# A decoder layer in float32: in the down projection, 19 low weight parts come from accumulating DMAs and 13 places, not 10, use Strassen's seven products

## The reference

```python
h = rms_norm(x); proj = h @ w_in                       # 2048 x 9216
y_a = multiscale_pool(...) @ w_branch_a
y_b = hgrn2(...) @ w_branch_b
x = x + (sigmoid(gate_a) * y_a + sigmoid(gate_b) * y_b) @ w_out
u = causal_depthwise_conv(rms_norm(x) @ w_up)          # 2 x 5504 columns
u_gate, u_val = split(u)
x = x + (silu(u_gate) * u_val) @ w_down                # 5504 x 2048: the down projection
x = x + sigmoid(rms_norm(x) @ w_ple_gate) * (p @ w_ple)
return rms_norm(x)
```

## Time and profile before

| | |
|---|---|
| median of 3 runs | 1424.06 us (1424.05 to 1424.47) |
| the profiled execution | 1424.01 us, of which the span is 1422.1 us |
| granted TensorE clock, mean | 0.998 of full |
| TensorE busy | 1412.8 us, 99% of the span |
| VectorE busy | 1070.7 us, 75% |
| ScalarE busy | 789.3 us, 56% |
| GpSimd busy | 133.6 us, 9% |
| HBM read | 270.53 MB, 192 GB/s over the span |

### The profile page before, as it was taken

How to read it: one execution, slowest core, us unless ns; L and a number is a source line. 1 busy time by engine, 2 the same in 40 slices (tenths; PEclk the granted TensorE clock), 3 DMA queues, 4 the chain that set the end, 5 groups by cost and what they waited for, 6 DMA issues and landing times.

```text
span 1422.1 us, 19817 instructions
## 1 busy us (share of the span) xinstructions
PE 1412.8 (99%) x7060; PEld 1200.5 (84%) x7060; DVE 1070.7 (75%) x1354; ACT 789.3 (56%) x959; POOL 133.6 (9%) x87
## 2 busy tenths in 40 slices
PE   9999999999999999999999999999999999999997
PEld 8888888888888888888888888888888888888886
DVE  7676777878787888777777777777777888887755
ACT  7565665555455555455555555555555555555544
POOL 0024123100000000001110111101111000000000
PEclk9999999999999999999999999999999999999999
DMA  9665554565666675475656556566665556565653
GB/s 327 198 182 160 169 185 149 164 191 176 196 210 186 216 239 195 152 222 178 200 177 198 187 182 197 179 199 184 185 194 181 201 193 206 172 218 191 233 199 120
DMA packets 190877, 273.48 MB, mean 192 GB/s; under 512 B 11744, under 2 KB 103136, under 8 KB 190688
## 3 DMA queue, kind: packets, MB, share of 16 engines
q1 hardware_dynamic: 190384, 272.30, 59.8%
q10 hardware_dynamic: 432, 0.37, 0.1%
HBM read 270.53 MB, written 2.10 MB: 192 GB/s over the span
## 4 chain that ended last, share of the span: by engine, by line
PE 98%; DVE 1%; issue 0%; ACT 0%; ACTq 0%; POOLq 0%; POOL 0%; DVEq 0%
PE aux L933 11%; PE main L933 11%; PE main L718 10%; PE main L720 10%; PE main L719 10%; PE aux L942 6%; PE main L942 6%; PE main L776 5%; PE main L777 5%; PE main L778 5%; PE aux L776 4%; PE aux L777 4%; PE aux L778 4%; PE aux L720 2%; PE aux L718 2%; PE aux L719 2%
## 5 line engine op out<-in xcount | busy, mean ns | idle before, releaser
L1552 DVE TENSOR_TENSOR w_lo<-raw,w_hi 128x1024 fp32r<-128x1024 f32 (+1 forms) x478 | 583.9, 1235 | 291.3 <-ACT w_hi L1226 290.2
L1226 ACT ACTIVATE w_hi<-raw 128x1024 fp32r<-128x1024 f32 (+1 forms) x478 | 501.4, 1051 | 462.8 <-PE main L720 126.8
L718 PE MATMUL main<-w_hi,xT 128*128 128x512 f32 x510 | 200.7, 394 | 0.0
L719 PE MATMUL main<-w_lo,xT 128*128 128x512 f32 x510 | 198.6, 389 | 0.0
L720 PE MATMUL main<-w_hi,xT 128*128 128x512 f32 x510 | 198.5, 389 | 0.0
L933 PE MATMUL aux<-xT,w_hi 128*128 128x512 f32 x704 | 169.7, 391 | 0.0
L933 PE MATMUL main<-xT,w_hi 128*128 128x512 f32 x672 | 162.8, 391 | 0.0
L933 PEld LDWEIGHTS aux<-xT,w_hi 128*128 128x128 f32 x704 | 129.4, 188 | 25.1
L933 PEld LDWEIGHTS main<-xT,w_hi 128*128 128x128 f32 x672 | 123.2, 188 | 23.6
L720 PEld LDWEIGHTS main<-w_hi,xT 128*128 128x128 f32 x510 | 95.7, 188 | 20.0
L718 PEld LDWEIGHTS main<-w_hi,xT 128*128 128x128 f32 x510 | 95.8, 188 | 19.7 <-DVE xT L1579 0.4
(11 more groups left out here) (347 smaller groups left out, 2167.7 us busy)
## 6 DMA issues: line engine op xcount, KB each, us to landing
raw<-in_w_up SPq DMA_DIRECT2D x336, 256.0 KB
raw<-in_w_in SPq DMA_DIRECT2D x136, 512.0 KB
raw<-in_w_down SPq DMA_DIRECT2D x84, 512.0 KB
raw<-in_w_out SPq DMA_DIRECT2D x32, 512.0 KB
raw<-in_w_ple_gate SPq DMA_DIRECT2D x32, 512.0 KB
raw<-in_w_branch_a SPq DMA_DIRECT2D x16, 512.0 KB
raw<-in_w_branch_b SPq DMA_DIRECT2D x16, 512.0 KB
raw<-in_w_in SPq DMA_DIRECT2D x15, 256.0 KB, 5.6
```

The lines of the kernel that those rows point to most:

```text
L718: pe.matmul(acc, th, wh, start=first, stop=False)
L719: pe.matmul(acc, th, wl, start=False, stop=False)
L1226: ac.activation(w_hi[:, u % RING, :, 0:w], raw[:, u % RING, :, 0:w], ACT.Copy).then_inc(hi_full, 1)
L1552: dve.tensor_tensor(w_lo[:, u % RING, :, 0:w], raw[:, u % RING, :, 0:w], w_hi[:, u % RING, :, 0:w].bitcast(F32), ALU.subtract).then_inc(lo ...
```

## The change

Three things change, all in the down projection. `SEVEN_AT` gets 13 places instead of 10. Of the plain units with a = 1, 19 (`LO_BY_DMA`: local numbers 13, 17, 19, 23, 27, 29, 33, 37, 39 and 53, 57, 59, 63, 67, 71, 73, 77, 81, 83) no longer get their low part from VectorE. For these, ScalarE first writes the negated high part into a buffer of its own, `w_lo_more`, two deep; then a DMA issued by GpSimd reads the same weights a second time from HBM and adds them onto it. TensorE waits for that DMA (`lo_arrived`). SyncE may refill the ring place of such a unit as soon as its high part is made. The size of a scratch area for the DMA descriptors of GpSimd is set, too.

```diff
-SEVEN_AT = ((5, 8, 11, 14, 17), (5, 8, 11, 14, 17))
+SEVEN_AT = ((5, 7, 10, 12, 15, 17), (3, 5, 8, 10, 12, 15, 17))
...
+LO_BY_DMA = [down_unit(p, i, 1) for p in range(2) for i in range(6 - 2 * p, 20) if i not in SEVEN_AT[p]]
+def lo_split(u):
+    return u + 1 - sum(v <= u for v in LO_BY_DMA)
...
+        w_lo_more = sb("w_lo_more", [P, 2, 2, NCOL], F32R, ffn)
...
+        def lo_arrived(eng, u, it=None):
+            if it is None and u in LO_BY_DMA:
+                k = LO_BY_DMA.index(u)
+                eng.wait_ge(hi_full, u + 1)
+                eng.wait_ge(lo_added[k % 2], 16 * (k // 2 + 1))
+            else:
+                eng.wait_ge(lo_full, plus(lo_split(u), 2 * UK, it))
...
             def slot_split(u, it=None):
                 if u >= RING:
-                    sp.wait_ge(lo_full, plus(u - RING + 1, 2 * UK, it))
+                    if it is None and u - RING in LO_BY_DMA:
+                        sp.wait_ge(hi_full, u - RING + 1)
+                    else:
+                        lo_arrived(sp, u - RING, it)
...
             def down_plain(u, p, i, a):
-                pe.wait_ge(lo_full, u + 1)
+                lo_arrived(pe, u)
...
             def split_hi(u, it=None):
                 ac.wait_ge(raw_full[u % RING], plus(32 * (u // RING + 1), 32 * (2 * UK // RING), it))
+                if it is None and u in LO_BY_DMA:
+                    k = LO_BY_DMA.index(u)
+                    if k > 1:
+                        ac.wait_ge(units_done, LO_BY_DMA[k - 2] + 1)
+                    ac.activation(w_lo_more[:, k % 2], raw[:, u % RING], ACT.Copy, scale=-1.0).then_inc(hi_negated, 1)
                 if u >= RING:
                     ac.wait_ge(units_done, plus(u - RING + 1, 2 * UK, it))
...
             def split_lo(u, it=None):
-                if u >= UNITS:
+                if u >= UNITS or (it is None and u in LO_BY_DMA):
                     return
...
+            for k, u in enumerate(LO_BY_DMA):
+                p, i = divmod((u - DOWN) // 2, UD)
+                pool.wait_ge(hi_negated, k + 1)
+                pool.dma_start(w_lo_more[:, k % 2], w_down_v[:, 2 * i:2 * i + 2, (2 * p + 1) * NCOL:(2 * p + 2) * NCOL],
+                               accum_op=ALU.add).then_inc(lo_added[k % 2], 16)
             root(2)
...
-    nc = bacc.Bacc("TRN2", target_bir_lowering=False, num_devices=1)
+    nc = bacc.Bacc("TRN2", target_bir_lowering=False, num_devices=1, dynamic_dma_scratch_size=8192)
```

More of the change, by code:

```diff
@@ L367, in build @@
         lo_full = sem("lo_full")
+        hi_negated, lo_added = sem("hi_negated"), [sem(f"lo_added{r}") for r in range(2)]
         units_done = sem("units_done")
@@ L722, in unit @@
             def unit(u, c, i, n, hi, lo, k, it=None, width=NCOL, tiles=2):
-                pe.wait_ge(lo_full, plus(u + 1, 2 * UK, it))
+                lo_arrived(pe, u, it)
                 for a in range(tiles):
@@ L787, in ring_tile @@
             def ring_tile(u, t):
-                return w_hi[:, u % RING, t, :], w_lo[:, u % RING, t, :]
+                low = w_lo_more[:, LO_BY_DMA.index(u) % 2, t, :] if u in LO_BY_DMA else w_lo[:, u % RING, t, :]
+                return w_hi[:, u % RING, t, :], low
             def sum_tile(q, t):
@@ L1186, in _ @@
                 for j in range(SPLIT_TB):
-                    pe.wait_ge(lo_full, u + j + 1)
+                    lo_arrived(pe, u + j)
                     for a in range(2):
@@ L1193, in _ @@
                     main_released(c - 1)
-                pe.wait_ge(lo_full, u + SPLIT_TB + 1)
+                lo_arrived(pe, u + SPLIT_TB)
                 if tb == 0:
```

## The result

The changed kernel takes 1473.88 us (median of 4 runs, 1469.45 to 1474.01) beside 1424.10 us for the kernel before: a ratio of 1.0341, 95% interval 1.0329 to 1.0354. That is 49.8 us slower, where 5 us slower was forecast. The profiled execution is the shortest of the four: 1469.45 us, a span of 1467.6 us, 45.4 us over the one before.

The account below looks back on a forecast made before the run. TensorE, busy 99%, alone was taken to bound the down projection. The terms -2.04 + 0.1 + 1.1 + 6.0 gave about +5 us on 1424.01, so 1429.1 us, range 1422.0 to 1440 (the forecast's own 1426.9 to 1437).

Parts of the forecast that it names:

- The accumulating DMA: the term that decides: Down projection, 19 units: DMA takes 6.0 us (4.1 load, 1.3 reading SBUF, 0.6 descriptors and sharing), adding +6.0 us in all.
- The upper bound of the same paragraph: Accumulating DMA behind or between two loads of a burst takes as long as three loads together, 8.3 us.
- The time that TensorE leaves: From negated copy to TensorE's start: 5.35 us at 13 units behind a place, 5.9 us at six second pairs.
- They don't add in full: Latenesses of 8.5 and 0.6 us partly overlap, as VectorE and loads gain during waits; two thirds kept, +6.0 us.
- the four units named beforehand: Units 17, 53, 57 and 71, where TensorE's largest waits for the accumulating DMA were expected; waits of 0.3 to 1.3 us.
- VectorE's load: Down projection: VectorE's total hardly moves, -2 us, but changed order costs 0.1 at one spot and +1.2 us together at others.
- in time: Rival: the DMA lands within 5.3 us at nearly all units; 1423.2 us, up to 1426.8, reading as no change; chance 0.38.
- The rival of a worse order: Rival: VectorE's new order leaves weight sums 1 us late at 13 places, +11 us, 1435; counted within the forecast's 0.43.
- TensorE's saving: Down projection: three more places save nine matmuls of 0.227 us each, -2.04 us, the most the change can give.
- GpSimd's and SyncE's edits at nothing: SyncE's earlier refill, the two buffers and GpSimd's other work in the down projection cost or gain nothing.
- the slow DMA: Rival: at triple DMA cost or slow descriptors, 7.5 to 9 us each, 1449 to 1466; with milder 7 us form, chance 0.16.
- The test that was set down beforehand: Prediction counts as wrong if TensorE doesn't wait for these DMAs, or waits over 1.5 us for each.

Follow-up runs that it names:

- the lighter loads: Changed kernel with its accumulating DMAs whole, but the down projection's ordinary weight loads fetch only one of two tiles (output wrong): 1447.39 us.
- the kernel kept busy: Changed kernel with 121 matmuls of zeros added on TensorE ahead of the seven long waits: 1463.11 us, ratio 1.0271 to the kernel before.
- the places alone: Changed kernel with its 13 places but no DMA from GpSimd, VectorE making all low parts again: 1431.95 us, ratio 1.0056 to the kernel before.
- Without any DMA: Changed kernel with its negated copies but without the 19 DMAs or TensorE's wait for them (output wrong): 1426.48 us, ratio 1.0017 to the kernel before.
- the plain copy: Changed kernel with the 19 GpSimd DMAs copying the weights without adding them (low parts wrong): 1447.65 us.
- the copy from ScalarE's queue: Changed kernel with ScalarE issuing a plain copy into an unread buffer in place of GpSimd's accumulating DMA (low parts wrong): 1440.33 us.

## Why the prediction was wrong

**The step that failed is "The accumulating DMA: the term that decides", its value of 6.0 us.** The mechanism was right: TensorE waits for this DMA behind the places. The size was that of a DMA alone. Measured alone it is 6.0 us indeed, with a split (3.5, 0.4 and 2.0) close to the terms of the prediction (4.1, 0.6, 1.3). In its place it takes 9.2, and in eleven of 19 cases its first packet comes 3.9 to 6.0 us behind the issue, not 1.9. The sentence "It lies nearer to the low end, since the queue is empty 40% of the time" took a mean over 229 us for a transfer that starts at much the same spot, just behind the weight differences that release the loads. While it runs the share is 0.76 to 1.00 (0.93 in the wait at unit 13), and at unit 13 SyncE has issued two loads ahead of it and two behind. What of the 3.2 us the loads' bytes don't explain (60%, by the lighter loads) stays open. The upper bound of the same paragraph, 8.3 us for three loads of a burst, was the row to go by: it describes the situation, and the 4.1 us does not.

**The time that TensorE leaves** (5.35 us for the 13 units, 5.9 for the six) held at seven of the 13, with 5.0 to 6.7 us from the issue (5.9 at unit 23). It did not hold elsewhere: 10.3 to 12.6 us at the six units that follow a stop, and 9.0 to 12.6 at the six second pairs, where the forecast had 5.9.

**"They don't add in full", two thirds kept**, had the right direction and the wrong size. With the time to landing measured, 9.2 - 5.35 is 3.85, and 0.3 from copy to issue makes 4.15 at 13 units; 3.6 at the six others; together 75.6 us. Two thirds of that are 50 us; 30.1 were measured, 0.40 of it. Put into the prediction's sum, 50 us would have given 1473 us, next to what was measured, but by chance: the factor too high would have stood in for the clock that was missing. The factor hid the form, too: 3.1 to 5.8 us at seven units, and next to nothing between. The largest waits are at 53, 13 and 71; two of the four units named beforehand (17 and 57) have none.

**A term was missing: TensorE's clock.** Behind each long stop the granted clock is 0.50, until 3.0 to 5.7 us behind TensorE's restart: 12.2 us by the rows, and 5.7 to 10.8 us of the total by the kernel kept busy. The prediction had waits of 0.3 to 1.3 us in mind, and waits of that size were not followed by it: the places alone have seven of 0.8 to 1.2 us and no matmul of the stage at the lower clock.

**VectorE's load, +1.2 us**, fits the changed kernel, where the rows show 1.1 us (unit 52, 0.3 to 0.5 us late for 0.4 worked out). In part that is luck: the stops give VectorE time. Without any DMA, the case that "in time" stood for, the order costs 4.4 us; units 16, 56 and 70, late there by 0.3 to 0.7, had not been looked at. The reason given for no more, that "VectorE's total hardly moves", is an argument from the mean again. The rival of a worse order (1 us late at each new place) does describe the places alone, seven times 1.0.

**TensorE's saving, -2.04 us**, held: nine matmuls less, 0.227 apart at full clock. **GpSimd's and SyncE's edits at nothing** held as far as the rows tell: no wait names them.

**Of the rivals** the slow DMA, 7.5 to 9 us and 1449 to 1466, came nearest in size and fell short by 8 us, with the factor too high and the clock missing. Its name, "the DMA engines become the bound", does not fit: the share of the stage is 0.71, and with lighter loads it falls to 0.55 while the DMA is still late. The 0.71 must not be read as the accumulation at the cost of a plain load, though, for which the prediction had worked out the same number: it is a share of 275 us, 195 us of the engines' time against 0.58 x 229.7 = 133 before, 62 more, where a plain second read of 10 MB on 45 would add 30. The addition nearly doubles the engines' work for these bytes (56 against 32 us by the queue rows), and the longer stage hides it. What bounds is the time of one DMA in its place among the loads. The test that was set down beforehand ("if it waits over 1.5 us for each") is met in sum, 30.1 us over 19 units, though ten of them have no wait.

## What to carry to other kernels

A transfer on a short path is priced by the stretch in which it runs, not by the stage's mean share: look at what the same event releases on the other queues, and take the row of a transfer inside such a burst. A share must be multiplied by the length of its stage before two kernels are compared. When a wait of several microseconds on TensorE can come out, add what its clock loses behind it. And before work is moved off an engine to make room for a saving, run the saving with the moved work left out: here that alone shows +2.4 us, so that no price of the transfer could have made the change a gain.

## What the runs showed of the hardware

- An accumulating DMA of 512 KB costs 2.0 us more than a plain one from the same engine (5.9 and 3.9 us), into float32r as into float32. GpSimd's issue of it is 1.20 us long, of the plain one 0.71 us.
- Its packets took 56 us of the DMA engines' time for 9.96 MB, those of the plain copy 32 us.
- A plain load of 512 KB takes 3.5 us alone (SyncE's queue) and 6.5 us (4.1 to 7.6) among the bursts of another queue (ScalarE's). The accumulating one's first packet came 1.9 us behind the issue alone and 5.2 us at unit 13, 3.7 us with the burst's loads halved, which took 1.3 us off the whole.
- In the changed kernel stops of 3.1 to 5.8 us on TensorE were each followed by a granted clock of 0.50, seven times in seven, until 3.0 to 5.7 us behind the restart; zero matmuls in the stop kept it at 1.00. The length of the stop alone doesn't decide: with the plain copy a stop of 3.5 us (unit 13) left the clock at 1.00, and with the copy from ScalarE's queue one of 2.2 us (unit 53) was followed by 0.50.
- GpSimd's subtraction of 128x512 beside VectorE's of the same shape stretched the latter from 0.68 to 1.78 us.
